# Down pass of an expert layer: another order of tile work, three buffers for split tiles, four for fetched rows, exponentials in pairs

## The chip, the cores and the metric

The kernel runs on one core of a Trainium2 chip. The metric is the device time of one execution in microseconds; a kernel is given by the median of several runs. The core's engines work in parallel, each in the order of its own program, and wait for each other on semaphores: TensorE (PE, matrix products and transposes through it), VectorE (DVE), ScalarE (ACT, activation functions), GpSimd (POOL, here the issue of gathers) and the queue of SyncE (SP, here loads). ScalarE and GpSimd issue DMAs too.

## The reference

One block of a network on 1024 tokens of width 1024: a normalised input goes through a projection, a gated recurrence and a state-space mixer, which are merged and added to the input. Then comes the expert layer, where the change lies:

```python
q = (xb @ w_q).reshape(t, PEER_HEADS, 2, PEER_HALF)
s = jnp.einsum('thpd,hpkd->thpk', q, sub_keys)
sv, si = lax.top_k(s, K)                       # K = 16 of 128 keys, twice
cand = sv[:, :, 0, :, None] + sv[:, :, 1, None, :]
cv, ci = lax.top_k(cand.reshape(t, PEER_HEADS, K * K), K)
idx = i1 * PEER_KEYS + i2                      # one of 16384 experts
g = jax.nn.softmax(cv, axis=-1)
act = jax.nn.gelu(jnp.einsum('thkd,td->thk', expert_down[idx], xb))
return jnp.einsum('thk,thkd->td', g * act, expert_up[idx])
```

Each token chooses 8 x 16 = 128 of 16384 experts. An expert is a row of 1024 numbers of the down table and one of the up table.

## The kernel before

The program is a series of stages with a barrier between them: vectors_and_norm, project_in, ssd, merge, post_mix, queries, experts_down, experts_up. The change is in experts_down (line 1750) and in the selection helpers (lines 1404 to 1503), which queries uses too.

Of the eight blocks of 128 tokens, five (640 tokens, TD) are treated densely and three (NA = 3, 384 columns of chosen rows) by gathers.

**The dense part of the down pass.** The down table is 128 tiles (E1) of 128 experts. For tile n, SP loads it into down_raw (two buffers); TensorE turns it with 8 transposes into ps_d (two buffers, `turn`, line 1873); ScalarE copies it rounded as the high half into downT_hi (`cut`, line 1928); VectorE subtracts that to get downT_lo (`low`, line 1996), each half with two buffers. TensorE then multiplies tile n with the tokens in two halves of 320 tokens (`products`, line 1880): 24 matmuls each, for high x high, high x low and low x high. The first half waits for low(n). ScalarE applies gelu to each half and stores it to scratch_gu, to be read by the up pass.

**Weight groups.** The dense part needs, for every expert and every token, the softmax weight. 160 groups of 4 tokens (QB) make them: ScalarE writes first_weighted (`first`, 4 Abs and 4 Relu activations), VectorE writes hit_second (`second`), TensorE multiplies them (`weights`, 8 instructions in the trace), and ScalarE copies the result out (`keep_weights`) and stores it later in pieces of 512 KB. first_weighted, hit_second and the result have two buffers each. Groups are spread over tiles 12 to 121, so one or two a tile; `granules_of(n)` gives those of tile n. At the start of each of the five token blocks `turn_picks` transposes the choices on TensorE, and VectorE copies them out.

**Selection.** While the tiles run, VectorE also picks the experts of 49 heads (HEADS): in even tiles `select_keys`, in odd ones `select_picks`. Each head needs an exponential with a sum on ScalarE (`select_act`), another table than gelu's; then `choose` on VectorE names the rows and multiplies by the reciprocal of the sum (line 1501, down_sel_inv). This ends with tile 98.

**Fetched rows.** GpSimd gathers 384 times 128 rows of the down table, 512 KB each, into down_rows with RING = 6 buffers (line 1867); VectorE makes a dot product with the tokens (`dot`, line 2007) and the buffer is free. 264 dots are spread over tiles 0 to 97, 2 or 3 a tile, and the last 120 over tiles 98 to 127, 4 a tile.

**The order on each engine**, by hand:
- TensorE, tile n: products half 0, turn(n+2), the groups of tile n, products half 1.
- ScalarE, tile n: gelu half 0; in every even tile one exponential; copies of the groups of n; gelu half 1; cut(n+2), which waits for half 1 of tile n; store of the gelu result; first_weighted of the groups of n+1; weight stores.
- VectorE, tile n: in even tiles choose for the head before; the dots; keys or picks; low(n+2); hit_second of the groups of n+1.
- SP: tile loads (each waits for the turn two before) and, every second tile, the scores of a head.

The up pass starts behind a barrier, when the stores have landed.

Of the kernel before, what the change touches and what calls it, by code (L numbers as in the profile page):

```python
# [41 lines left out]
NA = 3  # L42
# [1355 lines left out]
SEL_STEPS = 25  # L1398
# [5 lines left out]
def selection(m, st, tag):  # L1404


    b = {}
    for name, shape, dt in (("scores", [P, 2, 2, PK], F32), ("scores_rest", [P, 2, PK], F32), ("top", [P, 2, TOPK], F32),
                            ("idx", [P, 2, TOPK], U32), ("idx_f", [P, 2, TOPK], F32),
                            ("cand", [P, TOPK, TOPK], F32), ("cand_rest", [P, TOPK, TOPK], F32),  # L1410
                            ("cv", [P, TOPK], F32), ("ci", [P, TOPK], U32), ("ij", [P, 2, TOPK], U32),
                            ("ij_f", [P, 2, TOPK], F32), ("neg_max", [P, 1], F32), ("hit", [P, 2, TOPK, TOPK], F32),
                            ("pick", [P, 2, TOPK], F32),
                            ("exp", [P, TOPK], F32), ("exp_sum", [P, 1], F32), ("inv", [P, 1], F32)):
        b[name] = m.sb(st, f"{tag}_{name}", shape, dt)
    return b
# [27 lines left out]
def select_picks(dve, b, step, iota, n, keys):  # L1444
# [3 lines left out]
    idx = b["idx"]  # L1448
# [6 lines left out]
    dve.max(b["cv"][:, 0:8], flat(b["cand"])).then_inc(step, 1)  # L1455
    dve.tensor_copy(b["idx_f"][:], idx[:]).then_inc(step, 1)
    after(12)
    dve.max_index(b["ci"][:, 0:8], b["cv"][:, 0:8], flat(b["cand"])).then_inc(step, 1)
    dve.match_replace(flat(b["cand_rest"]), b["cv"][:, 0:8], flat(b["cand"]), -3.0e38).then_inc(step, 1)
    dve.tensor_scalar(b["neg_max"][:], b["cv"][:, 0:1], -1.0, None, ALU.mult).then_inc(step, 1)  # L1460
    after(15)
    dve.max(b["cv"][:, 8:16], flat(b["cand_rest"])).then_inc(step, 1)
    after(17)
    dve.max_index(b["ci"][:, 8:16], b["cv"][:, 8:16], flat(b["cand_rest"])).then_inc(step, 1)
# [16 lines left out]
def select_act(act, b, step, exp_done, n):  # L1481

    act.wait_ge(step, n * SEL_STEPS + 17)
    act.activation(b["exp"][:], b["cv"][:], ACT.Exp, bias=b["neg_max"][:], accum_out=b["exp_sum"][:]
                   ).then_inc(exp_done, 1)


def select_rows(dve, b, step, n, id_f, ids, named):
# [4 lines left out]
    dve.scalar_tensor_tensor(id_f, b["pick"][:, 0], float(PK), b["pick"][:, 1], ALU.mult, ALU.add).then_inc(named[0], 1)  # L1493
# [23 lines left out]
def queries(m, inp, keep, scratch):  # L1517
# [5 lines left out]
    with ExitStack() as st:  # L1523
# [28 lines left out]
        step, exp_done = m.sem("q_sel_step"), m.sem("q_sel_exp")  # L1552
# [6 lines left out]
        with nc.Block() as block:  # L1559
# [141 lines left out]
            def _(dve):  # L1701
# [18 lines left out]
                def choose(h, which):  # L1720
# [4 lines left out]
                    if which == 0:  # L1725
                        select_picks(dve, sel, step, iota, n, sel["pick"][:])
                        select_rows(dve, sel, step, n, row_f[:, 0, at], row_ids[:, 0, at], (rows_named, 2 * h + 1))
                        select_weights(dve, sel, step, exp_done, n, row_g[:, 0, at], head_chosen)
                    else:
                        select_picks(dve, sel, step, iota, n, chosen[:, 0, 1:3, at])  # L1730
                        select_weights(dve, sel, step, exp_done, n, chosen[:, 0, 0, at], head_chosen)
# [12 lines left out]
RING = 6  # L1744
# [5 lines left out]
def experts_down(m, inp, keep, scratch):  # L1750
# [13 lines left out]
    with ExitStack() as st:  # L1764
        raw = m.sb(st, "down_raw", [P, 2, D])
        d_hi = m.sb(st, "downT_hi", [P, 2, KD, P], F32R)
        d_lo = m.sb(st, "downT_lo", [P, 2, KD, P], F32R)
# [19 lines left out]
        step, exp_done = m.sem("d_sel_step"), m.sem("d_sel_exp")  # L1787
# [29 lines left out]
        def dots_of(n):  # L1817
# [3 lines left out]
            return range(early + (n - LATE) * 4, early + (n - LATE + 1) * 4)  # L1821

# [9 lines left out]
        with nc.Block() as block:  # L1832
# [39 lines left out]
            def _(pe):  # L1872
# [7 lines left out]
                def products(n, half):  # L1880
# [5 lines left out]
                    for k in range(KD):  # L1886
                        for d, h in ((d_hi, 0), (d_hi, 1), (d_lo, 0)):
                            mm = pe.matmul(ps_u[half][:, 0:HD], d[:, n % 2, k, :], h2[h][:, k, half * HD:(half + 1) * HD],  # L1888
# [25 lines left out]
                for n in range(E1):  # L1914
                    products(n, 0)
                    if n + 2 < E1:
                        turn(n + 2)
                    if n == W_FIRST - 4:
# [5 lines left out]
                    products(n, 1)  # L1924

            @block.scalar
            def _(act):
                def cut(n):
                    act.wait_ge(turned, n + 1)
                    if n >= 2:  # L1930
                        act.wait_ge(u_done[1], n - 1)
                    act.copy(d_hi[:, n % 2], ps_d[n % 2][:]).then_inc(hi_done, 1)
# [46 lines left out]
                for n in range(E1):  # L1979
                    gelu(n, 0)  # L1980
                    if n % 2 == 0 and 0 < n // 2 <= HEADS:
                        select_act(act, sel, step, exp_done, n // 2 - 1)
                    for g in granules_of(n):
                        keep_weights(g)
                    gelu(n, 1)
                    if n + 2 < E1:
                        cut(n + 2)
                    store(n)
                    for g in granules_of(n + 1):
                        first(g)  # L1990
                    for tile, piece in pieces_of(n):
# [3 lines left out]
            def _(dve):  # L1995
                def low(n):
                    dve.wait_ge(hi_done, n + 1)
                    dve.tensor_tensor(d_lo[:, n % 2], ps_d[n % 2][:], d_hi[:, n % 2].bitcast(F32), ALU.subtract  # L1998
# [11 lines left out]
                def keys_of(n):  # L2010
# [3 lines left out]
                    return sel["pick"][:] if b < NA else chosen[:, (b - NA) % 2, 1:3, at]  # L2014

                def choose(n):
# [5 lines left out]
                    select_weights(dve, sel, step, exp_done, n, row_g[:, b, at] if b < NA else chosen[:, (b - NA) % 2, 0, at],  # L2022
                                   head_chosen)
# [23 lines left out]
                for n in range(E1):  # L2047
                    s, odd = divmod(n, 2)
                    if not odd and 0 < s <= HEADS:
                        choose(s - 1)  # L2050
                    for c in dots_of(n):
# [6 lines left out]
                    if n + 2 < E1:  # L2058
                        low(n + 2)
# [387 lines left out]
```

## Time and profile before

| | us |
|---|---|
| median of 3 runs | 4403.21 (4396.81 to 4406.94) |
| profiled execution | 4395.88 |
| its span | 4394.1 |
| TensorE busy | 4031.5 (92%) |
| VectorE busy | 2552.7 (58%) |
| ScalarE busy | 1707.8 (39%) |
| GpSimd busy | 1803.1 (41%) |
| mean granted TensorE clock | 0.965 of full |

The down pass runs from about 1890 to 3280 us of the span. A busy TensorE is not one at its peak: its instructions overlap in the records, so the spacing of their starts says more than their durations. Shares of busy time are averages; what bounds a stage is read from the waits of that stage.

### The profile page before, as it was taken

To read this page: it belongs to the slowest core of one execution; us is meant where nothing else is said; L and a number is where in the kernel's file an instruction comes from. 1 tells how busy PE (TensorE), PEld (TensorE's weight loads), DVE (VectorE), ACT (ScalarE), POOL (GpSimd) and SP (SyncE) were. 2 spreads that over 40 slices of the span, in tenths; PEclk is the share of its full clock that TensorE was granted. 3 is DMA by queue.
4 is the path that set the end of the run, shared out by engine and by line. 5 is a ranking of instruction groups with operands and counts; after the bars stand their busy time and mean duration, and the time that the engine had idled before them with its cause. 6 is when DMAs were issued, how large, how long until landed. Compare 5 with 4: busy or idle time off the path is not lost. (4 is left out here: it accounts for less than half of the span.)

```text
span 4394.1 us, 62137 instructions
## 1 busy us (share of the span) xinstructions
PE 4031.5 (92%) x22397; PEld 3345.2 (76%) x22428; DVE 2552.7 (58%) x4790; ACT 1707.8 (39%) x3262; POOL 1803.1 (41%) x1278
## 2 busy tenths in 40 slices
PE   8899999899789879988888888888979999999998
PEld 4688878678677669978888888888976776766676
DVE  3455311145565425688878888887665555555555
ACT  2123343344322331136767677676632222122212
POOL 0333333245343302133323333334546666666664
PEclk9999999999899889989999999999999999999999
DMA  7223333244455242166777778779999999999997
GB/s 288 54 87 98 102 100 96 93 109 129 136 170 189 72 137 63 52 241 212 236 234 237 238 238 254 232 248 306 324 325 339 329 324 330 335 325 325 332 336 276
DMA packets 637601, 939.50 MB, mean 214 GB/s; under 512 B 198692, under 2 KB 416180, under 8 KB 637364
## 3 DMA queue, kind: packets, MB, share of 16 engines
q1 hardware_dynamic: 319412, 408.93, 28.7%
q0 software_dynamic: 110592, 402.70, 25.9%
q10 hardware_dynamic: 207360, 124.80, 9.1%
q8 instruction: 138, 2.26, 0.2%
q14 instruction: 99, 0.81, 0.1%
HBM read 790.55 MB, written 145.75 MB: 213 GB/s over the span
## 5 line engine op out<-in xcount | busy, mean ns | idle before, releaser
L1867 POOL DMA_INDIRECT down_rows<-in_peer_down_dram,row_ids x384 | 499.1, 1300 | 932.7 <-DVE row_u L2007 802.9
L1888 PE MATMUL p_u<-h2T_hi,downT_hi 128*128 128x320 f32 x2048 | 655.1, 320 | 3.8 <-DVE downT_lo L1998 3.8
L1888 PE MATMUL p_u<-h2T_lo,downT_hi 128*128 128x320 f32 x2048 | 641.8, 313 | 0.0
L1888 PE MATMUL p_u<-h2T_hi,downT_lo 128*128 128x320 f32 x2048 | 641.1, 313 | 0.0
L2155 POOL DMA_INDIRECT up_rows<-in_peer_up_dram,row_ids_turned x384 | 416.9, 1086 | 242.0 <-PE p_rows L2318 146.9
L2357 PE MATMUL p_y<-up_hi,coef_hi 128*128 128x512 f32 x1240 | 494.9, 399 | 1.1 <-DVE coef_lo L2252 1.1
L2007 DVE CUSTOM_DVE_ANT_0 gate_rows<-down_rows,x_tok_rows 128x1024 f32<-128x1024 f32 x384 | 469.4, 1223 | 38.9 <-DMA down_rows<-in_peer_down_dram,row_ids 1.8
L2357 PE MATMUL p_y<-up_lo,coef_hi 128*128 128x512 f32 x1240 | 485.5, 392 | 0.0
L2357 PE MATMUL p_y<-up_hi,coef_lo 128*128 128x512 f32 x1240 | 482.7, 389 | 0.0
L2262 DVE TENSOR_TENSOR y_acc<-p_y,y_acc 128x512 f32<-128x512 f32 x310 | 211.2, 689 | 376.7 <-PE p_y L2357 376.7
L514 PE MATMUL p<-hT_hi,w_hi 128*128 128x512 f32 x1024 | 405.0, 396 | 0.0
L1888 PEld LDWEIGHTS p_u<-h2T_hi,downT_hi 128*128 128x128 f32 x2048 | 395.1, 193 | 5.6 <-DVE downT_lo L1998 5.6
L514 PE MATMUL p<-hT_hi,w_lo 128*128 128x512 f32 x1024 | 398.8, 389 | 0.0
L514 PE MATMUL p<-hT_lo,w_hi 128*128 128x512 f32 x1024 | 398.6, 389 | 0.0
L1888 PEld LDWEIGHTS p_u<-h2T_lo,downT_hi 128*128 128x128 f32 x2048 | 394.4, 193 | 0.0
L1888 PEld LDWEIGHTS p_u<-h2T_hi,downT_lo 128*128 128x128 f32 x2048 | 392.6, 192 | 0.0
L2162 POOL TENSOR_TENSOR up_lo<-up_raw,up_hi 128x1024 fp32r<-128x1024 f32 x128 | 305.9, 2403 | 114.1 <-ACT up_hi L2198 112.8
L2357 PEld LDWEIGHTS p_y<-up_hi,coef_hi 128*128 128x128 f32 x1240 | 232.5, 188 | 127.2 <-issue 52.0
L1908 PE MATMUL p_w<-first_weighted,hit_second 128*128 128x128 f32 x1280 | 193.6, 299 | 143.5 <-issue 81.2
L2200 ACT CAST coef_hi<-gelu_in 128x640 fp32r<-128x640 f32 x128 | 93.2, 728 | 571.5 <-DVE gelu_in L2250 571.5
L1908 PEld LDWEIGHTS p_w<-first_weighted,hit_second 128*128 128x128 f32 x1280 | 165.5, 203 | 170.9 <-ACT first_weighted L1959 90.2
L2357 PEld LDWEIGHTS p_y<-up_hi,coef_lo 128*128 128x128 f32 x1240 | 232.8, 188 | 50.9
(349 smaller groups left out, 8176.5 us busy)
## 6 DMA issues: line engine op xcount, KB each, us to landing
down_raw<-in_peer_down_dram SPq DMA_DIRECT2D x128, 512.0 KB, 4.3
up_raw<-in_peer_up_dram SPq DMA_DIRECT2D x128, 512.0 KB, 5.7
scratch_gu<-gelu_out ACTq DMA_DIRECT2D x128, 320.0 KB, 5.2
gelu_in<-scratch_gu SPq DMA_DIRECT2D x128, 320.0 KB, 4.7
weights_in<-scratch_w SPq DMA_DIRECT2D x128, 320.0 KB, 6.8
w_raw<-in_w_in_dram SPq DMA_DIRECT2D x64, 512.0 KB, 4.1
w_ada_sb<-in_w_ada_dram SPq DMA_DIRECT2D x12, 2048.0 KB, 15.3
scratch_w<-weights_out ACTq DMA_DIRECT2D x40, 512.0 KB, 6.4
```

The costliest lines, as they stand in the source:

```text
L514: mm = pe.matmul(ps[u][:, half, :], w[:, u, k, :], hT[h][:, k, half * TH:(half + 1) * TH], start=(n == 0), stop=(n == 3 * KD - 1))
L1867: pool.indirect_dma_start(out=rows[:, c % RING, :], out_offset=None, in_=inp["peer_down"][0], in_offset=bass.IndirectOffsetOnAxis(ap=row_i ...
L1888: mm = pe.matmul(ps_u[half][:, 0:HD], d[:, n % 2, k, :], h2[h][:, k, half * HD:(half + 1) * HD], start=(j == 0), stop=(j == 3 * KD - 1))
L1908: mm = pe.matmul(ps_w[g % 2][:, t, :], b_[:, g % 2, t, :], a_[:, g % 2, t, :], start=(t == 0), stop=(t == QB - 1), skip_group_check=True)
L2007: dve.tensor_tensor_reduce(junk, rows[:, c % RING, :], x_tok[:, a], 1.0, 0.0, ALU.mult, ALU.add, row_u[:, a, k:k + 1]).then_inc(dot_done, 1)
L2155: pool.indirect_dma_start(out=rows[:, n % SETS, j, :], out_offset=None, in_=inp["peer_up"][0], in_offset=bass.IndirectOffsetOnAxis(ap=ids_ ...
L2162: pool.tensor_tensor(up_lo[:, g % 2, j, :], up_raw[:, u], up_hi[:, g % 2, j, :].bitcast(F32), ALU.subtract).then_inc(up_lo_done, 1)
L2200: act.copy(g_hi[:, v, j, :], gu[:, u]).then_inc(g_hi_done, 1)
L2262: dve.tensor_tensor(part, ps_y[s % BANKS][:], part, ALU.add).then_inc(added, 1)
L2357: mm = pe.matmul(ps_y[s % BANKS][:], a[:, v, j, t * P:(t + 1) * P], b[:, v, j, half * TH:(half + 1) * TH], start=(n == 0), stop=(n == 3 * ...
```

## The change

1. downT_hi and downT_lo get three buffers (n % 3), so that cut(n) waits for half 1 of tile n-3 and not of n-2. RING becomes 4, so the gather of row c waits for the dot of row c-4.
2. TensorE: the groups of tile n stand behind products half 1.
3. ScalarE: gelu half 0, cut(n+2), gelu half 1, store, copies of the groups of n, first_weighted of the groups of n+1, then, in every fourth tile, the exponentials of two heads, then weight stores.
4. VectorE: half of the dots (rounded down), low(n+2), in every fourth tile choose for two heads, the other dots, keys or picks, name_rows (part of choose before), hit_second of the groups of n+1.
5. The values that live longer (cv, neg_max, pick, exp, exp_sum, inv) get two buffers, and the reciprocal a semaphore of its own; SEL_STEPS goes from 25 to 24. The same helpers are used in queries, in the same order as before.

```diff
-                            ("cv", [P, TOPK], F32), ("ci", [P, TOPK], U32), ("ij", [P, 2, TOPK], U32),
...
+                            ("cv", [P, 2, TOPK], F32), ("ci", [P, TOPK], U32), ("ij", [P, 2, TOPK], U32),
...
-def select_weights(dve, b, step, exp_done, n, weight, chosen):
+def select_weights(dve, b, exp_done, inv_done, n, weight, chosen):
...
+    u = n % 2
     dve.wait_ge(exp_done, n + 1)
-    dve.reciprocal(b["inv"][:], b["exp_sum"][:]).then_inc(step, 1)
-    dve.wait_ge(step, n * SEL_STEPS + 25)
-    dve.tensor_scalar(weight, b["exp"][:], b["inv"][:], None, ALU.mult).then_inc(chosen, 1)
+    dve.reciprocal(b["inv"][:, u:u + 1], b["exp_sum"][:, u:u + 1]).then_inc(inv_done, 1)
+    dve.wait_ge(inv_done, n + 1)
+    dve.tensor_scalar(weight, b["exp"][:, u], b["inv"][:, u:u + 1], None, ALU.mult).then_inc(chosen, 1)
...
-RING = 6
+RING = 4
...
-        d_hi = m.sb(st, "downT_hi", [P, 2, KD, P], F32R)
-        d_lo = m.sb(st, "downT_lo", [P, 2, KD, P], F32R)
+        d_hi = m.sb(st, "downT_hi", [P, 3, KD, P], F32R)
+        d_lo = m.sb(st, "downT_lo", [P, 3, KD, P], F32R)
...
+        def ended_in(n):
+            pair = (n - 3) // 4
+            return range(2 * pair, min(2 * pair + 2, HEADS)) if n >= 3 and n % 4 == 3 else range(0)
...
                     products(n, 0)
                     if n + 2 < E1:
                         turn(n + 2)
+                    products(n, 1)
                     if n == W_FIRST - 4:
                         turn_picks(0)
                     for g in granules_of(n):
                         if (g + 1) % IN_BLOCK == 0 and g + 1 < GRANULES:
                             turn_picks((g + 1) // IN_BLOCK)
                         weights(g)
-                    products(n, 1)
...
                     act.wait_ge(turned, n + 1)
-                    if n >= 2:
-                        act.wait_ge(u_done[1], n - 1)
-                    act.copy(d_hi[:, n % 2], ps_d[n % 2][:]).then_inc(hi_done, 1)
+                    if n >= 3:
+                        act.wait_ge(u_done[1], n - 2)
+                    act.copy(d_hi[:, n % 3], ps_d[n % 2][:]).then_inc(hi_done, 1)
...
                     gelu(n, 0)
-                    if n % 2 == 0 and 0 < n // 2 <= HEADS:
-                        select_act(act, sel, step, exp_done, n // 2 - 1)
+                    if n + 2 < E1:
+                        cut(n + 2)
+                    gelu(n, 1)
+                    store(n)
                     for g in granules_of(n):
                         keep_weights(g)
-                    gelu(n, 1)
-                    if n + 2 < E1:
-                        cut(n + 2)
-                    store(n)
                     for g in granules_of(n + 1):
                         first(g)
+                    for head in ended_in(n):
+                        select_act(act, sel, step, exp_done, head)
                     for tile, piece in pieces_of(n):
                         store_weights(tile, piece)
...
-                    if not odd and 0 < s <= HEADS:
-                        choose(s - 1)
-                    for c in dots_of(n):
+                    todo = dots_of(n)
+                    for c in todo[:len(todo) // 2]:
+                        dot(c)
+                    if n + 2 < E1:
+                        low(n + 2)
+                    for head in ended_in(n - 1):
+                        choose(head)
+                    for c in todo[len(todo) // 2:]:
                         dot(c)
                     if s < HEADS and not odd:
                         dve.wait_ge(s_loaded[s % 2], 16 * (s // 2 + 1))
                         select_keys(dve, sel, step, s)
                     if s < HEADS and odd:
                         select_picks(dve, sel, step, iota, s, keys_of(s))
-                    if n + 2 < E1:
-                        low(n + 2)
+                        name_rows(s)
                     for g in granules_of(n + 1):
                         second(g)
```

## Rows read from the trace of the kernel before

**Rows 1.** Windows of the down pass, transposes of line 1877: stretch, its us, busy (count), clock, DMA share, GB/s
```profile
1893.00:2998.00 1105.00, 103.59 (x800) 93.09 (x800) 0.96 0.76 241
2998.00:3227.00 229.00, 22.78 (x176) 20.50 (x176) 0.99 0.96 319
3227.00:3273.00 46.00, 4.14 (x32) 3.73 (x32) 1.00 1.03 352
```
**Rows 2.** The same for the weight groups' matmuls, line 1908
```profile
1893.00:2998.00 1105.00, 156.49 (x1024) 134.49 (x1024) 0.96 0.76 241
```
**Rows 3.** Waits of TensorE and of VectorE, 1893 to 2998: total us, times, longest
```profile
PE p_w L1908 <- issue: 81.2, 56, 2.2
PE p_w L1908 <- ACT first_weighted L1959: 41.5, 24, 9.1
...
DVE down_sel_inv L1501 <- ACT down_sel_exp L1484: 122.3, 45, 4.3
DVE downT_lo L1998 <- ACT downT_hi L1932: 15.0, 11, 3.6
```
**Rows 4.** Timeline of TensorE, second and third stage: start us, us, instruction, [idle before]
```profile
3034.40 1.03 PE L1877 MATMUL p_down<-ident,down_raw 128*128 128x128 f32 x8
...
3043.35 1.03 PE L1877 MATMUL p_down<-ident,down_raw 128*128 128x128 f32 x8
...
3047.12 1.16 PE L1908 MATMUL p_w<-first_weighted,hit_second 128*128 128x128 f32 x8 [1.69 <-ACT first_weighted L1959]
...
3055.16 1.04 PE L1877 MATMUL p_down<-ident,down_raw 128*128 128x128 f32 x8
...
3230.38 1.03 PE L1877 MATMUL p_down<-ident,down_raw 128*128 128x128 f32 x8
...
3238.29 1.03 PE L1877 MATMUL p_down<-ident,down_raw 128*128 128x128 f32 x8
```
**Rows 5.** Timeline of ScalarE, VectorE, TensorE around one exponential of the first stage
```profile
2508.95 1.28 ACT L1484 ACT_TABLE_LOAD   x1
2510.25 0.31 ACT L1484 ACTIVATE down_sel_exp<-down_sel_cv,down_sel_neg_max 128x16 f32<-128x16 f32 x1
...
2510.68 0.16 DVE L1501 RECIPROCAL down_sel_inv<-down_sel_exp_sum 128x1 f32<-128x1 f32 x1 [4.33 <-ACT down_sel_exp L1484]
...
2512.40 1.22 DVE L2007 CUSTOM_DVE_ANT_0 gate_rows<-down_rows,x_tok_rows 128x1024 f32<-128x1024 f32 x1
...
2513.77 1.23 DVE L2007 CUSTOM_DVE_ANT_0 gate_rows<-down_rows,x_tok_rows 128x1024 f32<-128x1024 f32 x1
...
2514.92 0.48 DVE L1429 MAX8 down_sel_top<-down_sel_scores 128x8 f32<-128x128 f32 x2
...
2519.13 0.68 DVE L2042 TENSOR_TENSOR hit_second<-picks_turned_sb,iota_row 128x512 f32<-128x512 f32 x1
...
2519.91 1.23 PE L1908 MATMUL p_w<-first_weighted,hit_second 128*128 128x128 f32 x8 [2.16 <-issue]
```
**Rows 6.** Timeline of ScalarE: the first activations of two groups in a row
```profile
3041.26 1.28 ACT L1954 ACTIVATE first_weighted<-iota_row,picks_turned_sb 128x128 f32<-128x128 f32 x4
...
3044.13 1.26 ACT L1954 ACTIVATE first_weighted<-iota_row,picks_turned_sb 128x128 f32<-128x128 f32 x4
```
**Rows 7.** Tile down_rows, gathers in the first, second, third stage
```profile
DMA to landing us min/median/max: 4.8/6.3/9.5
...
DMA to landing us min/median/max: 5.1/6.8/8.0
...
DMA to landing us min/median/max: 5.9/7.9/8.8
```
**Rows 8.** Timeline at the end: last dot, last weight stores, first load of the up pass
```profile
3271.89 1.23 DVE L2007 CUSTOM_DVE_ANT_0 gate_rows<-down_rows,x_tok_rows 128x1024 f32<-128x1024 f32 x1 [0.17 <-DMA down_rows<-in_peer_down_dram,row_ids]
...
3273.68 3.70 ACTq L1974 DMA_DIRECT2D scratch_w<-y_acc  x3
...
3282.57 0.33 SPq L2124 DMA_DIRECT2D up_raw<-in_peer_up_dram  x1
```

More of the change, by code:

```diff
@@ L1397 @@
 HP = 2 * PH
-SEL_STEPS = 25
+SEL_STEPS = 24
 SCORES_READ = 6
@@ L1444, in select_picks @@
 def select_picks(dve, b, step, iota, n, keys):
-    idx = b["idx"]
+    idx, cv = b["idx"], b["cv"][:, n % 2]
     def after(k):
@@ L1492, in select_rows @@
     dve.wait_ge(step, n * SEL_STEPS + 24)
-    dve.scalar_tensor_tensor(id_f, b["pick"][:, 0], float(PK), b["pick"][:, 1], ALU.mult, ALU.add).then_inc(named[0], 1)
+    dve.scalar_tensor_tensor(id_f, b["pick"][:, n % 2, 0], float(PK), b["pick"][:, n % 2, 1], ALU.mult, ALU.add).then_inc(named[0], 1)
     dve.wait_ge(named[0], named[1])
     dve.tensor_copy(ids, id_f).then_inc(named[0], 1)
-def select_weights(dve, b, step, exp_done, n, weight, chosen):
+def select_weights(dve, b, exp_done, inv_done, n, weight, chosen):
+    u = n % 2
     dve.wait_ge(exp_done, n + 1)
-    dve.reciprocal(b["inv"][:], b["exp_sum"][:]).then_inc(step, 1)
-    dve.wait_ge(step, n * SEL_STEPS + 25)
-    dve.tensor_scalar(weight, b["exp"][:], b["inv"][:], None, ALU.mult).then_inc(chosen, 1)
+    dve.reciprocal(b["inv"][:, u:u + 1], b["exp_sum"][:, u:u + 1]).then_inc(inv_done, 1)
+    dve.wait_ge(inv_done, n + 1)
+    dve.tensor_scalar(weight, b["exp"][:, u], b["inv"][:, u:u + 1], None, ALU.mult).then_inc(chosen, 1)
 def expert_keep(m, stack, keep):
@@ L1887, in products @@
                         for d, h in ((d_hi, 0), (d_hi, 1), (d_lo, 0)):
-                            mm = pe.matmul(ps_u[half][:, 0:HD], d[:, n % 2, k, :], h2[h][:, k, half * HD:(half + 1) * HD],
+                            mm = pe.matmul(ps_u[half][:, 0:HD], d[:, n % 3, k, :], h2[h][:, k, half * HD:(half + 1) * HD],
                                            start=(j == 0), stop=(j == 3 * KD - 1))
@@ L2013, in keys_of, with name_rows @@
                     at = slice(h * TOPK, (h + 1) * TOPK)
-                    return sel["pick"][:] if b < NA else chosen[:, (b - NA) % 2, 1:3, at]
-                def choose(n):
+                    return sel["pick"][:, n % 2] if b < NA else chosen[:, (b - NA) % 2, 1:3, at]
+                def name_rows(n):
                     b, h = heads[n]
@@ L2021, in choose @@
                                     (rows_named, 2 * fetched_heads.index((b, h)) + 1))
-                    select_weights(dve, sel, step, exp_done, n, row_g[:, b, at] if b < NA else chosen[:, (b - NA) % 2, 0, at],
-                                   head_chosen)
+                def choose(n):
+                    b, h = heads[n]
+                    at = slice(h * TOPK, (h + 1) * TOPK)
+                    select_weights(dve, sel, exp_done, inv_done, n,
+                                   row_g[:, b, at] if b < NA else chosen[:, (b - NA) % 2, 0, at], head_chosen)
                 def keep_picks(w):
```

32 lines of the change are left out of this document (16 added, 16 removed).

## The prediction

> **What bounds the kernel now.** I read the windows first, for the stages of the down pass. It has three: 1105 us with selection running beside the products (TensorE clock 0.96, DMA share 0.76), 229 us without selection but with four fetched rows a tile (clock 0.99, DMA 0.96), and 46 us of bare tiles at the end (DMA 1.03) [rows 1]. A turn of one tile is 8 transposes, so the counts give 800/8 = 100, 22 and 4 turns; the tile period is 11.05 us in the first stage and 10.4 us in the second. 1024/8 = 128 of the 160 weight groups lie in the first [rows 2], 32 in the second.
>
> Then the timeline of TensorE in the quieter second stage, for what a tile costs if nobody waits: a tile without a group takes 3238.29 - 3230.38 = 7.91 us, one with a single group 3043.35 - 3034.40 = 8.95, so a group costs 1.04. A tile with two takes 3055.16 - 3043.35 = 11.81 instead of 10.0, because its second group waits 1.69 us for ScalarE's first_weighted [rows 4]. TensorE's own work in the first stage is therefore 100 x 7.91 + 128 x 1.04 = 924 us of 1105.
>
> Third the waits. TensorE's idle time in the first stage is nearly all in front of the weight groups (81.2 us under "issue", 41.5 us for first_weighted); VectorE waits 122.3 us for the softmax exponential and 15.0 us for the high half of a tile, and hardly anything else [rows 3]. The rest of VectorE's stage, 1105 - 122 - 15 = 968 us, is work and its small gaps. So the stage is not bound by one engine but by a loop: TensorE half 0 -> gelu -> table load and exponential -> VectorE dots, keys, low half, hit_second -> TensorE's group. One turn of it is seen whole [rows 5]: the table load starts at 2508.95, the exponential at 2510.25, VectorE can take the reciprocal only at 2510.68, does its dots (2512.40, 2513.77) and keys (2514.92), writes hit_second at 2519.13 for 0.68 us, and TensorE, idle for 2.16 us, starts the group at 2519.91. That wait is marked "issue" but ends 0.1 us after hit_second: it is VectorE's lateness.
>
> All times are of the profiled execution (4395.9 us, span 4394.1); it lies 7 us under the median of the three runs, 4403.2.
>
> **The change part by part.**
>
> *Groups behind both halves, ScalarE reordered.* Before, a group is wanted 3.5 + 0.9 us into its tile (half a product, the turn); after, at 7.9 us. ScalarE begins first_weighted when the previous tile's last group has been copied out (0.6 us into the tile) and needs 3044.13 - 3041.26 = 2.87 us for a group [rows 6]: two are ready at 0.6 + 5.7 = 6.3 us, before 7.9. Both the 1.69 us wait of the second stage and the ScalarE waits of the first have cover then. hit_second has 3.5 us more too. Instructions and DMAs are the same in number; the stores of gelu results go earlier past the groups and the store of weights stays last. If the cover were gone the price is again 1.7 us for a tile with two groups.
>
> *Third buffer of the split tile.* cut(n+2) waited for half 1 of tile n; now for half 1 of tile n-1. It can run at 4.4 us into tile n (end of its turn) instead of 7.9. By itself this buys nothing where low has a tile of slack, but it lets ScalarE and VectorE do the cut before their long work. What is late next is ScalarE itself: cut sits behind the previous tile's first_weighted, so it ends near 5.5 us into the tile with one group ahead and near 7.8 us with two.
>
> *Exponentials in pairs.* 49 heads cause 49 detours through the tables, now 25. A detour of one head is a load of 1.28, the exponential's 0.31 and a load back, taken as long; of two heads it is about 3.3 us [rows 5]. ScalarE gains about 60 us over the pass, off the path. The point is the order: choose stands behind low(n+3), and low needs a cut which ScalarE issues after the exponentials, so the 122 us wait cannot recur at choose. It can reappear as a wait for the cut: in a tile with exponentials the cut ends at about 8.2 us (one group) or 11.1 us (two). A VectorE that is itself the last engine comes to low at 7.9 + 1.2 = 9.1 us, so only the second case waits, 2.0 us, in some 10 of the 22 tiles with exponentials and groups: +20 us.
>
> The Trainium skill bears on this (page "ScalarE: Activation LUTs", section "What ACT_TABLE_LOAD costs"): it gives a drain of about 1.38 us beside the 1.28 us of each load. In the trace the load and the exponential stand 1.30 us apart and no drain shows [rows 5]. With the page's drain the pair's detour would be an estimated 2.8 us longer, and the stage's sum about 35 us higher; the row decides, and I do not add it.
>
> *Dots split around low.* A dot behind another starts after 1.37 us (2512.40 to 2513.77), the last of a run lets the next operation start after 1.15 (2513.77 to 2514.92) [rows 5]: a dot waits 0.22 us for the one before. Two runs a tile instead of one save 0.22 x 98 = 22 us of VectorE. name_rows moves up by one iteration, so row numbers are ready earlier; reciprocals and multiplies are the same.
>
> First stage then: TensorE 924 us at full clock, VectorE 968 - 22 = 946 us. VectorE is the bound. Add 20 us for cuts behind exponentials and 8 us for the four times that the picks are turned (VectorE and ScalarE have to wait for a turn which now stands at the tile's end, about 2 us each; my estimate, between 0 and the 2.9 us of a group). That is 974, taken as **970 us: -135**. From below the bound is VectorE's 946 (-160); from above, half of its 137 us of waits stay (1035, -70). TensorE's clock rises with it: it is 0.99 where waits are 1.7 us and 0.96 where they are longer, and at 0.97 its work is 953 us, still beside VectorE's.
>
> Second stage: TensorE's floor is 22 x 7.91 + 32 x 1.04 = 207 us. The transfers are 229 us x 319 GB/s = 73.1 MB; at the 352 GB/s which the last stage moves they take 207 us too [rows 1]. Two limits at one spot meet above it; I take 9.8 us a tile, 215 us: **-14** (0 to -22).
>
> *Four buffers for fetched rows.* A buffer is busy from the GpSimd issue (0.15 us after the dot) to landing, and for the dot: 6.3 + 1.5 = 7.8 us in the first stage (up to 11.0 with the slowest landing, 9.5), 8.3 in the second, 7.9 + 1.5 = 9.4 in the last [rows 7]. In the first stage the fourth dot back is at least a tile (9.7) away: hidden, and lost in full on VectorE if landing passes about 9. In the second four rows a tile fit 9.8 us, barely. In the last they don't fit 7.9: VectorE falls behind 1.5 us a tile, 9 us at the end less the 1.4 us or more it now idles in each of those tiles. At the end ScalarE issues weight stores until 3277.4 and the up pass loads at 3282.6, 9 us after the last dot [rows 8]: **+1** (0 to +9).
>
> Sum: -135 - 14 + 1 = -148, so 4395.9 - 148 = 4248 us for an execution like the profiled one, and with the 7 us between it and the median, **4255 us**.
>
> **The rivals.**
> A: *the wait moves to the handshakes.* ScalarE's pair of exponentials, placed behind first_weighted, holds gelu and cut; VectorE waits for the cut in most tiles, not in 10. For it: ScalarE does all of it in series, and its parts are long [rows 5, 6]. Against it: two groups, an exponential pair, gelus and the cut come to about 11 us only in the fullest tiles; others leave it 3 us and more. Half of 137 us stays, so about -70 - 10: 4323.
> B: *rows come late.* Periods fall to 9.7 us, DMA share in the first stage rises to 0.76 x 11.05/9.7 = 0.87, landings go toward 9.5 us. The second stage then runs at 11.0 us a tile (+26 us against 9.8), the last at 11.0 (+10), and VectorE loses 0.5 us a tile in the first (+50): 4340. For it: landing rises from 6.3 to 7.9 us as the DMA share rises. Against: at share 0.96 its median is 6.8 still.
> C, slower: *four buffers throttle the whole pass.* 2.7 dots a tile need (landing + 1.5) x 2.7/4 us. That passes 11.05 us from a landing of 14.9 us on. At 16 it is 11.8 a tile and 17.5 with four rows: +75 +190, 4660. The longest landing seen is 9.5.
> D: *no effect*, if exponentials and groups only swap one wait for another of the same length: 4400. TensorE's 130 us of waits in front of groups would have to stand again, behind 3.5 us more cover.
>
> **How the numbers follow.** Forecast 0.72, A 0.13, B 0.08, C 0.04, D 0.03. The forecast's own range is 4220 to 4295 (VectorE's bound with -22 in the second stage, to half of the small terms missed). The range goes to 4335 to take in A and most of B, leaving C, D and what lies under 4218. A change under 0.2% (9 us) cannot be told from none. Faster 0.94, same 0.02, slower 0.04.
>
> **What would show it.** The exponential's wait at the reciprocal gone (122 to under 5 us); waits before the weight groups under 40 us in the first stage; VectorE busy over 0.9 of it; its wait for the cut 15 to 60 us; 50 table loads in the pass, not 98; clock 0.98 or more; a period of 9.7 us, and 9.8 in the second stage. Waits of VectorE for fetched rows only in the last tiles. It is wrong if VectorE idles for cuts or rows in most tiles (A, B), or if TensorE still waits a microsecond or more a tile before the groups.

## The result

The changed kernel takes 4267.8 us in the median (4264.4 to 4274.2), the kernel before 4403.4: a ratio of 0.9695, 95% interval 0.9679 to 0.9712. The forecast was 4255 us, within 4218 to 4335. Its profiled execution spans 4264.9 us against 4394.1, 129.2 less, where my sum said 148. One execution of e12 below took 8499.4 us, twice the others, and is left out of its ratio; nothing here shows why.

To place the difference I cut both traces at the same landmarks, the starts of TensorE's turns: turn 2 (near the pass's start), turn 102 (selection over), turn 124 (weight groups over), the first load of the up pass. Every kernel below is cut in this way, from the timeline of TensorE.

| stretch of the profiled execution, us | before | after | change | forecast |
|---|---|---|---|---|
| start to turn 2 | 1897.7 | 1903.3 | +5.6 | 0 |
| turn 2 to 102, with selection | 1103.2 | 982.7 | -120.5 | -135 |
| turn 102 to 124, four rows a tile | 229.5 | 208.6 | -20.8 | -14 |
| turn 124 to the up pass | 52.2 | 60.2 | +8.1 | +1 |
| up pass | 1111.5 | 1110.0 | -1.5 | 0 |

Most of the 5.6 us at the start is not the change's. TensorE's first turn starts 5.1 us later than in the profiled execution of before, but 3.6 and 3.7 us later in two kernels below (e8, e3) that leave everything ahead of the down pass as it was, and 0.9 to 5.8 us later in the others.

The windows of the changed kernel, to set beside [rows 1]; columns: stretch, its length, busy time (count) of TensorE, its weight loads, VectorE, ScalarE and GpSimd, then clock, DMA share, GB/s:

```profile
1903.30:2886.00 982.70, 926.52 (x6641) 912.65 (x6640) 909.94 (x2533) 683.24 (x1596) 320.69 (x270) 0.99 0.85 268
2886.00:3094.60 208.60, 204.19 (x1490) 202.41 (x1489) 149.06 (x232) 149.99 (x358) 105.52 (x88) 1.00 1.01 348
3094.60:3154.90 60.30, 42.96 (x298) 42.14 (x296) 37.03 (x57) 9.32 (x16) 25.88 (x23) 0.88 1.01 332
```

VectorE is busy for 910 of 983 us, 0.93 of the stage; the clock is 0.99, not 0.96. The waits of the first stretch, against [rows 3]:

```profile
PE p_w L1915 <- issue: 29.4, 31, 1.7
PE p_w L1915 <- ACT first_weighted L1966: 14.4, 6, 7.3
PE p_u L1895 <- ACT gelu_out L1945: 8.6, 10, 2.7
...
DVE downT_lo L2005 <- ACT downT_hi L1939: 44.1, 23, 5.8
DVE gate_rows L2014 <- DMA down_rows<-in_peer_down_dram,row_ids: 2.6, 3, 1.6
```

The exponential's 122.3 us are gone from the list; TensorE's waits in front of groups fell from 122.7 to 43.8 us (I had asked for under 40). VectorE's wait for the cut, 15.0 us before, is now 44.1 us in 23 places. Part of it is the price of the detour through the tables with two exponentials. One tile shows it on ScalarE and VectorE (to be set beside [rows 5]):

```profile
2531.37 1.28 ACT L1485 ACT_TABLE_LOAD   x1
2532.67 0.31 ACT L1485 ACTIVATE down_sel_exp<-down_sel_cv,down_sel_neg_max 128x16 f32<-128x16 f32 x1
...
2533.38 1.28 ACT L1945 ACT_TABLE_LOAD   x1
2534.67 0.44 ACT L1945 ACTIVATE gelu_out<-p_u 128x320 f32<-128x320 f32 x1
2535.01 1.01 ACT L1939 CAST downT_hi<-p_down 128x1024 fp32r<-128x1024 f32 x1
...
2536.05 1.23 DVE L2005 TENSOR_TENSOR downT_lo<-p_down,downT_hi 128x1024 fp32r<-128x1024 f32 x1 [2.19 <-ACT downT_hi L1939]
```

The detour lasts from 2531.37 to 2534.67, 3.3 us; VectorE waits 2.19 us for the cut behind it. Both were in the forecast (3.3 and 2.0).

But not all 23 waits are of this kind. Sorted by what ScalarE did just ahead of each cut, 13 of them, 18.0 us, stand behind a pair of exponentials alone. Four, 16.4 us, stand behind a wait of ScalarE for turned picks that VectorE has yet to copy out (two of these have a pair as well); here is the first:

```profile
2008.06 1.28 ACT L1961 ACTIVATE first_weighted<-iota_row,picks_turned_sb 128x128 f32<-128x128 f32 x4 [11.76 <-DVE picks_turned_sb L2043]
...
2014.66 1.01 ACT L1939 CAST downT_hi<-p_down 128x1024 fp32r<-128x1024 f32 x1
...
2015.70 1.23 DVE L2005 TENSOR_TENSOR downT_lo<-p_down,downT_hi 128x1024 fp32r<-128x1024 f32 x1 [5.82 <-ACT downT_hi L1939]
```

Two waits, 5.6 us, are in the pass's first tiles, and four, 4.1 us, in tiles where ScalarE stood idle for about 3 us at the issue of a store.

TensorE's timeline shows one thing that I had not taken into account:

```profile
2835.70 1.03 PE L1884 MATMUL p_down<-ident,down_raw 128*128 128x128 f32 x8
2840.10 1.95 PE L1915 MATMUL p_w<-first_weighted,hit_second 128*128 128x128 f32 x16
2845.40 1.03 PE L1884 MATMUL p_down<-ident,down_raw 128*128 128x128 f32 x8
2849.80 1.05 PE L1915 MATMUL p_w<-first_weighted,hit_second 128*128 128x128 f32 x8
2854.20 1.04 PE L1884 MATMUL p_down<-ident,down_raw 128*128 128x128 f32 x8
```

A tile with two groups takes 2845.40 - 2835.70 = 9.70 us, with one 2854.20 - 2845.40 = 8.80: beside the 7.91 us of a tile without, a group costs 0.89 us, not the 1.04 of [rows 4]. The 1.69 us wait for a second group is gone.

At the end, the last dots and weight stores (against [rows 8]):

```profile
3148.70 1.22 DVE L2014 CUSTOM_DVE_ANT_0 gate_rows<-down_rows,x_tok_rows 128x1024 f32<-128x1024 f32 x1 [0.85 <-DMA down_rows<-in_peer_down_dram,row_ids]
3151.18 1.23 DVE L2014 CUSTOM_DVE_ANT_0 gate_rows<-down_rows,x_tok_rows 128x1024 f32<-128x1024 f32 x1 [1.25 <-DMA down_rows<-in_peer_down_dram,row_ids]
...
3138.82 9.65 ACTq L1981 DMA_DIRECT2D scratch_w<-y_acc  x3
...
3154.90 0.33 SPq L2139 DMA_DIRECT2D up_raw<-in_peer_up_dram  x1
```

The last dot ends at 3152.4 us, 14.5 us after TensorE's last product (3137.9 us), and the up pass begins 2.5 us behind it; before, the dot was 9 us ahead of the up pass. VectorE waits 19.8 us for rows in these 60 us, and 52.4 us already in the stage ahead with four rows a tile. I had expected such waits in the last tiles only. In the stage with four rows they lie in time that VectorE spent waiting for the cut before (66.3 us).

### The profile page after: what moved, and what is told of

Its sections match the earlier page's. It is cut to its first block and busy times, and to the rows that moved or that the text cites. A ratio compares the mean times of both kernels' runs of the same rounds, so it can differ in the third digit from the quotient of the medians.

```text
span 4264.9 us, 62088 instructions
## 1 busy us (share of the span) xinstructions
PE 3990.5 (94%) x22397; PEld 3317.1 (78%) x22428; DVE 2542.5 (60%) x4790; ACT 1654.5 (39%) x3214; POOL 1759.6 (41%) x1278
## 5 line engine op out<-in xcount | busy, mean ns | idle before, releaser
L1874 POOL DMA_INDIRECT down_rows<-in_peer_down_dram,row_ids x384 | 457.0, 1190 | 848.5 <-DVE row_u L2014 755.5
L2372 PEld LDWEIGHTS p_y<-up_lo,coef_hi 128*128 128x128 f32 x1240 | 232.8, 188 | 45.5
L1966 ACT ACTIVATE first_weighted<-first_weighted,picks_turned_sb 128x128 f32<-128x128 f32 x640 | 264.5, 484 | 5.3
## 6 DMA issues: line engine op xcount, KB each, us to landing
w_ada_sb<-in_w_ada_dram SPq DMA_DIRECT2D x12, 2048.0 KB, 15.1
```

What stands on the lines that cost most here:

```text
L1874: pool.indirect_dma_start(out=rows[:, c % RING, :], out_offset=None, in_=inp["peer_down"][0], in_offset=bass.IndirectOffsetOnAxis(ap=row_i ...
L1966: hit = act.activation(a_[:, g % 2, t, :], a_[:, g % 2, t, :], ACT.Relu, bias=picks[:, w % 2, 0, c:c + 1], scale=picks[:, w % 2, 1, c:c + 1])
L2372: mm = pe.matmul(ps_y[s % BANKS][:], a[:, v, j, t * P:(t + 1) * P], b[:, v, j, half * TH:(half + 1) * TH], start=(n == 0), stop=(n == 3 * ...
```

## The experiments

Theory: the place of the weight groups carries the gain, and VectorE's own time, with each of its waits and gaps, bounds the selection stage after it. Rivals: the pairs or the third buffer carry it; TensorE or the handshakes are the bound. And for the last stretch: the ring of four against a full DMA. The table has each kernel's stretches in us, its median, and its ratio to the kernel before on the same chip. "Rows" are the buffers for fetched rows.

| kernel | turn 2 to 102 | 102 to 124 | to up pass | median | ratio (95%) |
|---|---|---|---|---|---|
| before | 1103.2 | 229.5 | 52.2 | 4403.4 | |
| changed | 982.7 | 208.6 | 60.2 | 4267.8 | 0.9695 (0.9679 to 0.9712) |
| e1 five rows, low half two buffers | 988.9 | 207.5 | 54.7 | 4268.5 | 0.9701 (0.9688 to 0.9714) |
| e2 two buffers, six rows | 1013.6 | 210.1 | 54.1 | 4296.1 | 0.9759 (0.9746 to 0.9772) |
| e3 before, four rows | 1099.0 | 229.4 | 57.0 | 4403.8 | 1.0008 (0.9999 to 1.0017) |
| e4 single exponentials | 1000.2 | 206.7 | 60.7 | 4280.5 | 0.9726 (0.9711 to 0.9741) |
| e5 groups between halves | 1114.6 | 221.2 | 56.8 | 4407.4 | 1.0011 (1.0002 to 1.0021) |
| e6 dots unsplit | 975.1 | 207.1 | 58.7 | 4257.7 | 0.9672 (0.9651 to 0.9692) |
| e7 two buffers, four rows | 1017.1 | 206.8 | 59.2 | 4296.9 | 0.9759 (0.9743 to 0.9775) |
| e8 order alone | 986.8 | 203.8 | 52.2 | 4259.0 | 0.9677 (0.9660 to 0.9693) |
| e9 e8, choose later | 962.7 | 208.0 | 52.2 | 4235.3 | 0.9614 (0.9601 to 0.9627) |
| e10 e9, pairs | 965.9 | 203.0 | 52.5 | 4233.9 | 0.9617 (0.9604 to 0.9631) |
| e11 e10, three buffers, four rows | 965.0 | 206.7 | 61.5 | 4245.7 | 0.9640 (0.9626 to 0.9654) |
| e12 e10, dots apart | 945.6 | 204.8 | 54.2 | 4220.7 | 0.9583 (0.9571 to 0.9595) |

**e5, groups between the halves again** (the rest of the change kept)

```diff
                     products(n, 0)
                     if n + 2 < E1:
                         turn(n + 2)
-                    products(n, 1)
...
                         weights(g)
+                    products(n, 1)
...
+                    for g in granules_of(n):
+                        keep_weights(g)
                     gelu(n, 1)
                     store(n)
-                    for g in granules_of(n):
-                        keep_weights(g)
```

> The changed kernel with the weight groups back between the two halves on TensorE (and their copies back ahead of gelu half 1 on ScalarE); three buffers, pairs, split dots stay. Theory (the place of the groups gives the cover): four-row stage back from 209 to 225 to 230 us, selection stage from 983 to 1030 to 1080, total 4335 to 4385. Rival (pairs and the third buffer carry the gain): under +30 us in all.

The whole gain is gone: ratio 1.0011, where I had expected 4335 to 4385 us. The stage with four rows keeps 8 us of its gain (221.2 us), and the selection stage is 11 us longer than before. Its waits in the selection stage show the old picture without the exponential:

```profile
PE p_w L1915 <- issue: 73.8, 39, 3.8
PE p_w L1915 <- ACT first_weighted L1966: 55.7, 31, 10.8
...
DVE downT_lo L2005 <- ACT downT_hi L1939: 163.6, 66, 5.8
```

TensorE waits 130 us at the groups, as before (122.7), and VectorE has swapped its 122 us for the exponential for 164 us at the cut. Pairs, third buffer and split dots buy nothing without the cover.

This kernel also tells whether the place of a group sets what it costs TensorE. The group stands between the turn and products half 1 again:

```profile
3017.98 1.03 PE L1884 MATMUL p_down<-ident,down_raw 128*128 128x128 f32 x8
3018.85 1.06 PE L1915 MATMUL p_w<-first_weighted,hit_second 128*128 128x128 f32 x8
...
3026.78 1.04 PE L1884 MATMUL p_down<-ident,down_raw 128*128 128x128 f32 x8
```

The tile takes 8.80 us, as in the changed kernel, and so do most of its tiles with one group and no wait. The place doesn't set the cost. In the kernel before, the first two of a group's 8 instructions start 0.05 and 0.10 us later than here; the views call a gap a wait only from 0.15 us on.

**e8, the order alone**, made from the kernel before

```diff
+                    products(n, 1)
                     if n == W_FIRST - 4:
                         turn_picks(0)
...
                         weights(g)
-                    products(n, 1)
...
-                    for g in granules_of(n):
-                        keep_weights(g)
                     gelu(n, 1)
                     if n + 2 < E1:
                         cut(n + 2)
                     store(n)
+                    for g in granules_of(n):
+                        keep_weights(g)
```

> The kernel before with only the groups moved behind both halves on TensorE and their copies behind gelu half 1 and the cut on ScalarE; two buffers, ring of six, one exponential in each even tile at its old place, VectorE as before. Theory (the place gives the cover for ScalarE's and VectorE's lateness): four-row stage 229 to 208 to 212 us, selection stage 1103 to 1030 to 1050 (VectorE still waits 122 us for exponentials but bound by it), total 4320 to 4345. Rival (place alone does nothing while VectorE waits for the exponential): selection stage above 1080.

Better than the theory had it (4320 to 4345 us, selection stage 1030 to 1050): 4259.0 us and 986.8, at least as fast as the whole change (the intervals overlap, its end is 8 us shorter).

```profile
DVE down_sel_inv L1501 <- ACT down_sel_exp L1484: 24.3, 16, 4.3
DVE downT_lo L1998 <- ACT downT_hi L1932: 3.6, 1, 3.6
```

The wait for the exponential falls from 122.3 to 24.3 us with the exponentials where they were: most of it was a consequence of the loop, not a cost by itself. My reading is that with cover at the groups VectorE may run late, and comes to choose when the exponential is done.

**e4, single exponentials, and e10, pairs on the old places.** e4 changes one line of the changed kernel:

```diff
-            pair = (n - 3) // 4
-            return range(2 * pair, min(2 * pair + 2, HEADS)) if n >= 3 and n % 4 == 3 else range(0)
+            return range(n // 2, min(n // 2 + 1, HEADS)) if n >= 1 and n % 2 == 1 else range(0)
```

> The changed kernel with the exponential of each head at the end of each odd tile instead of two heads every fourth tile; everything else, place and order too, as changed. Theory (VectorE bound, pairs save only ScalarE time off the path): selection stage +5 to +20 us on 983 (more tiles in which the cut is late), total 4273 to 4288. Rival (the table loads are on the path: 24 detours of 2.6 us saved are the gain): +50 us or more.

It costs 12.7 us in the median and 17.5 in the selection stage, within the theory's range; VectorE's wait for the cut rises from 44.1 to 62.1 us. e10 (shown against the changed kernel, with two buffers as in e2 below) has pairs, but cut behind gelu half 1 and low at the end of the tile, against e9 with singles:

> The order-alone kernel with the exponentials in pairs at the end of every fourth tile, choose for both ahead of the last dot; two buffers, ring of six, cut behind gelu half 1 and low at the end of the tile, so of the change everything but the third buffer, the smaller ring and the early cut. Theory (pairs save ScalarE 60 us off the path and their wait is covered): within 6 us of the kernel with late choose and single exponentials. Rival (pairs carry a gain of their own, as the 12 us between singles and pairs in the full change suggest): 8 to 20 us faster than that kernel. Second rival (a pair's 3.3 us hold ScalarE up ahead of gelu): slower by 5 to 15.

```diff
-RING = 4
+RING = 6
...
                     gelu(n, 0)
+                    gelu(n, 1)
                     if n + 2 < E1:
                         cut(n + 2)
-                    gelu(n, 1)
...
-                    for c in todo[:len(todo) // 2]:
+                    for c in todo[:-1]:
                         dot(c)
-                    if n + 2 < E1:
-                        low(n + 2)
                     for head in ended_in(n - 1):
                         choose(head)
-                    for c in todo[len(todo) // 2:]:
+                    for c in todo[-1:]:
                         dot(c)
...
                         name_rows(s)
+                    if n + 2 < E1:
+                        low(n + 2)
```

There pairs make no difference (4233.9 against 4235.3 us). They matter only where the cut stands behind them and VectorE is waiting.

**e2 and e7, two buffers; e11, three buffers on the old places.** e2 and e7 take the buffers of the changed kernel from three to two (n % 2, wait for half 1 of tile n-2), with a ring of six and of four.

```diff
-        d_hi = m.sb(st, "downT_hi", [P, 3, KD, P], F32R)
-        d_lo = m.sb(st, "downT_lo", [P, 3, KD, P], F32R)
+        d_hi = m.sb(st, "downT_hi", [P, 2, KD, P], F32R)
+        d_lo = m.sb(st, "downT_lo", [P, 2, KD, P], F32R)
...
-                    if n >= 3:
-                        act.wait_ge(u_done[1], n - 2)
+                    if n >= 2:
+                        act.wait_ge(u_done[1], n - 1)
```

> The changed kernel with both halves back on two buffers and six row buffers: only the third buffer and the ring are undone. My theory holds that the third buffer is worth little, because VectorE comes to its low half at about 9 us into the tile and the cut is then ready at 8.9 us either way: selection stage +0 to +10 us on 983, last stretch back to 52 to 54; total 4260 to 4272. Rival (the early cut is what lets ScalarE and VectorE keep up): selection stage +30 us or more, total 4290 or more.

> The changed kernel with both halves on two buffers and four row buffers, so that against the changed kernel only the third buffer differs, and against the one with six row buffers only the ring. Expected with a weak third buffer: selection stage +0 to +10 us, last stretch 60 us, total 4268 to 4280; if the third buffer matters, +30 us or more.

Here I was wrong (I had given the stage 0 to 10 us): without the third buffer the selection stage is 31 and 34 us longer, 4296 and 4297 us. ScalarE's program explains it: with two buffers the cut, which stands ahead of gelu half 1, has to wait for half 1 of the same tile. In e2:

```profile
ACT downT_hi L1939 <- PE p_u L1895: 174.3, 72, 4.3
...
DVE downT_lo L2005 <- ACT downT_hi L1939: 73.3, 45, 8.1
```

and VectorE, with low in the middle of its tile, waits 73 us. e11 asks whether the buffer has a worth of its own, with cut and low late (e10 with three buffers and RING = 4):

> The kernel with pairs on the old places of cut and low (median 4234) with three buffers for both halves and four row buffers: the changed kernel, but cut behind gelu half 1, low at the end of the tile and dots in one run around choose. Theory (the early places of cut and low make the third buffer necessary; by itself it buys nothing): selection stage within 5 us of 966, last stretch 57 to 60 instead of 52.5 from the smaller ring, total 4234 to 4244. Rival (the third buffer or the smaller ring costs in itself what the changed kernel lacks): 4255 or more.

Selection stage 965.0 against e10's 965.9: none. The third buffer only pays for the early places of cut and low. The end is 9 us longer (61.5), more than I gave the ring, and the total 1.7 us above my upper bound.

**e6, dots in one run ahead of low**

```diff
-                    for c in todo[:len(todo) // 2]:
+                    for c in todo:
                         dot(c)
...
-                    for c in todo[len(todo) // 2:]:
-                        dot(c)
```

> The changed kernel with all dots of a tile ahead of the low half, in one run. If VectorE's own time bounds the selection stage, the 0.22 us gap more in each of 98 tiles shows: +10 to +25 us there (983 to about 1000), and in the four-row stage little. Rival (VectorE has slack, the stage is bound by the handshakes): within 5 us in the selection stage.

Wrong sign: 4257.7 us, the selection stage 7.6 us shorter. VectorE's wait for the cut fell from 44.1 to 16.3 us: the run of dots ahead of low is cover for the cut, and worth more than the gaps that the split saves. Against e11 (965.0), where cut and low stand late and choose ahead of the last dot, this kernel's stage is still 10 us longer.

**e9, choose later** (on e8)

```diff
-                    if not odd and 0 < s <= HEADS:
-                        choose(s - 1)
-                    for c in dots_of(n):
+                    todo = dots_of(n)
+                    for c in todo[:-1]:
+                        dot(c)
+                    if not odd and 0 < s <= HEADS:
+                        choose(s - 1)
+                    for c in todo[-1:]:
                         dot(c)
```

> The order-alone kernel (groups behind both halves, nothing else of the change) with choose moved from ahead of the tile's dots to ahead of its last dot. There VectorE waits 24 us for exponentials in the selection stage. Theory (VectorE is the bound now, so each wait and each gap of it counts): that wait falls under 8 us, the 0.22 us gap between two dots goes in half of the tiles (11 us), the stage falls from 987 to 955 to 970, total 4230 to 4248. Rival (the stage is bound by TensorE and the handshakes with ScalarE): within 5 us of the order-alone kernel's 4259.

4235.3 us, 24 less than e8; the stage falls by 24.1 us. The wait for the exponential went from 24.3 to 12.2 us (I had said under 8). Adjacent pairs of dots went from 171 to 123, and 48 x 0.22 us is 10.6: together about 23 us, and the stage follows VectorE's time one to one.

**e12, dots apart** (against e10), the fastest kernel here

```diff
-                    for c in todo[:-1]:
+                    for c in todo[:1]:
                         dot(c)
                     for head in ended_in(n - 1):
                         choose(head)
-                    for c in todo[-1:]:
-                        dot(c)
...
                         name_rows(s)
+                    for c in todo[1:2]:
+                        dot(c)
                     if n + 2 < E1:
                         low(n + 2)
+                    for c in todo[2:]:
+                        dot(c)
```

> The kernel with pairs on the old places of cut and low (median 4234) with the dots apart: one at the tile's start, one behind keys or picks, the rest behind low, so that hardly a dot follows a dot. Theory (VectorE's own time bounds the selection stage): up to 0.22 us a dot less, about 25 to 35 us of VectorE work; TensorE's floor of about 915 us then stands close, so the stage falls from 966 to 940 to 955, total 4208 to 4225. Rival (the stage is already bound by TensorE): within 5 us of 4234.

4220.7 us, as the theory said, and a further 20 us in the selection stage. The edit also moves choose and low, so I split the stage into VectorE's waits and the rest, its own time with the short gaps, summed from the traces:

| kernel | adjacent pairs of dots | VectorE's own time | its waits |
|---|---|---|---|
| before | 171 | 960.3 | 142.9 |
| changed | 72 | 936.0 | 46.7 |
| e6 | 171 | 956.4 | 18.8 |
| e10 | 148 | 953.8 | 12.1 |
| e12 | 11 | 924.0 | 21.6 |

From e10 to e12 there are 137 pairs fewer; 137 x 0.22 = 30 us, and VectorE's own time falls by 29.8. Its waits take 9.5 us back, the one for the exponential alone 8.1 to 17.6 us. So the gaps are worth 30 us here, of which a third is lost again to a wait. TensorE's waits at the groups are down to 9.6 us:

```profile
PE p_u L1895 <- ACT gelu_out L1945: 13.2, 13, 2.4
PE p_w L1915 <- ACT first_weighted L1966: 7.3, 3, 5.1
...
PE p_w L1915 <- issue: 2.3, 4, 0.8
```

**e1 and e3, the ring.** e1 gives the changed kernel five row buffers and the low half two (low then waits for half 1 of tile n-2's products); e3 is the kernel before with RING = 4.

```diff
-RING = 4
+RING = 5
...
-        d_lo = m.sb(st, "downT_lo", [P, 3, KD, P], F32R)
+        d_lo = m.sb(st, "downT_lo", [P, 2, KD, P], F32R)
...
                     dve.wait_ge(hi_done, n + 1)
+                    if n >= 2:
+                        dve.wait_ge(u_done[1], n - 1)
```

> The changed kernel with five row buffers, paid for by giving the low half (not the high half) two buffers again. Theory (four row buffers starve VectorE in the last tiles, 8 us from the last four turns to the up pass's first load, 60.2 against 52.2 us before): that stretch falls back to 52 to 55 us, VectorE's waits for rows after the selection fall from 74 us to under 35, the rest stays; total 4260 to 4264 in the median. Rival (the transfers themselves are full there, 343 GB/s at a share near 1, and what is won before is given back): stretch stays at 58 to 61 us, total within 3 us of the changed kernel's 4268. If the low half's third buffer mattered, the selection stage would be over 5 us longer.

> The kernel before with four row buffers and nothing else. If the last stretch's 8 us come from the ring: it goes from 52.2 to 58 to 61 us here too, the selection stage (1103 us) and the stage with four rows (229 us) within 5 us, total 4409 to 4416. Rival (the ring is harmless at the old pace): total within 3 us of 4403.

In e1 the last stretch falls to 54.7 us and VectorE's waits for rows behind the selection from 72.2 to 15.1 us, as the ring theory has it, but the total does not move (forecast 4260 to 4264): low now waits 16.2 us for products, and the selection stage gives 6.2 us back. In e3 the last stretch rises by 4.8 us, less than the 6 to 9 forecast. The total, forecast at 4409 to 4416, is 4403.8, 0.08% above the kernel before with an interval that takes in no change, so here the rival's total came true and the theory shows in the stretch alone. The smaller ring costs about 5 us at the end at the old pace, 5 from e2 to e7, and 9 from e10 to e11.

## Why the prediction was right, and where it missed

- *The loop, and the cover behind both halves: right.* e5 and e8 show it from both sides. I had not drawn the conclusion that the order alone would do: the 122 us at the exponential were counted as a wait that pairing had to remove, and e8 removes 98 of them without it.
- *TensorE's work, 924 us: too high.* A group costs 0.89 us: 100 x 7.91 + 128 x 0.89 = 905. The 1.04 that I read in [rows 4] holds 0.15 us of short gaps, which e5 does not have at the same place.
- *Second stage, -14: mis-sized, measured -20.8.* Its floor is 22 x 7.91 + 32 x 0.89 = 203 us, not 207, and I had added 8 us above it for two limits that meet. The 352 GB/s that I took as the second limit were none: e8 moves 362 there and takes 203.8 us.
- *VectorE's work, 946 us: about right.* 982.7 - 44.1 - 2.6 = 936.
- *Waits for the cut: the step that was mis-sized, but not at the exponentials.* All such waits are 44 us, where the sum had 20 for the exponentials and 8 for the turned picks. Behind a pair alone there are 13 of 18.0 us in all, against some 10 of 2.0 us: right. The four with turned picks cost VectorE 16.4 us, twice the 8; I had looked at the turn on TensorE, while ScalarE waits up to 11.8 us for VectorE's copy of the picks. The 5.6 us in the first tiles and 4.1 us at stores were not in the sum. So the 14.5 us missing in the stage are 16 more at the cut, 2.6 of waits for rows, 4 that I rounded off and 1.8 by which the stage of [rows 1] is longer than the one here, less 10 by which VectorE's work came out lower.
- *Dots split, -22 us: wrong as a gain.* The gaps are saved (99 adjacent pairs fewer, and 20.4 us less of VectorE's own time than in e6), but the split also brings low forward, ahead of its cut, and the waits rise by 27.9: the step costs 8 us in the stage. I costed the gaps and the cut's wait as independent.
- *Third buffer, nothing by itself: right (e11)*, but low has no slack in the new order, and there the buffer is needed (e2, e7: 28 and 29 us in the median).
- *Exponentials off the path: right where cut and low are late (e10), not in the changed kernel (e4: 12.7 us).*
- *Table loads, 3.3 us for a pair: right.* The drain that the Trainium skill gives (page "ScalarE: Activation LUTs", section "What ACT_TABLE_LOAD costs") shows in no row here either: 2531.37 + 1.28 = 2532.65, and the exponential starts at 2532.67.
- *Ring of four, +1 us: mis-sized*, the stretch is 8 us longer, inside the bounds given (0 to +9). VectorE falls behind by 14.5 us, not by 9, and the 9 us between last dot and up pass do not hide it.
- *Rivals.* A did not happen: VectorE waits for cuts in 23 of 100 tiles. B did not: from issue to landing a gather takes 5.9 us in the median in the selection stage (6.3 before), and VectorE waits 2.6 us for rows there. C and D did not.

The sum of 148 against 129: 5.6 us lost at the start, 14.5 us too much forecast for the selection stage, 6.8 too little for the one with four rows, 7.1 lost in the last stretch, and 1.5 won in the up pass. The forecast total came as near as it did partly by luck, since the second stage's extra gain makes up for the last stretch.

What stays open: what holds a group's first two instructions up by 0.15 us in the kernel before; how much of TensorE's gain comes with its clock (0.96 before, 0.99 after, in the selection stage); and what a larger ring alone would give the changed kernel, since e1 took a buffer from the low half too. The groups' places on TensorE and ScalarE were only moved together.

## What to carry to other kernels

When several engines wait on each other in a loop, look for the consumer that asks earliest for what is made latest, and put it behind other work: here this one move gave the whole gain, and made most of a wait vanish that had looked like a cost of its own. After it another engine is the bound, and there each wait and even each 0.2 us gap counts, unless another wait takes up what it frees. So apply the next edits one by one: the others together gained nothing here, and the split of the dots took away the cover of the cut. A copy moved early needs its own buffer and its own cover: measured with the move, the buffer looks worth 30 us, without the move nothing. And before a long wait is put down to its most visible cause, look at what stood ahead of each one.

## What the runs showed of the hardware

A group of 8 fp32 instructions of 128 columns costs TensorE 0.89 us, both between products (the changed kernel, e8) and between the transposes of a turn and products (e5); in the kernel before it cost 1.04 in that same place.

Adjacent dot products on VectorE, each of which waits for the one before, start 1.37 us apart, while another operation follows a dot after 1.15 us. With 137 adjacent pairs fewer among the same dots VectorE's own time fell by 29.8 us, and the kernel's median by 13 us (4220.7 against 4233.9), since other waits grew.

The table load of 1.28 us is followed by the exponential after 0.02 us.
